# Two gated networks: 12 of 22 gate/up units as seven block products, the gate-up product kept in float32

## The reference, cut to what matters

```
def swiglu(x, wg, wu, wd):
    return (jax.nn.silu(x @ wg) * (x @ wu)) @ wd

h = h + 0.5 * swiglu(rmsnorm(h, ffn1_norm), ffn1_wg, ffn1_wu, ffn1_wd)
...                                             # mixer: attention
h = h + 0.5 * swiglu(rmsnorm(h, ffn2_norm), ffn2_wg, ffn2_wu, ffn2_wd)
gate = jax.nn.sigmoid(rmsnorm(h, ple_gate_norm) @ ple_w_gate)
e = rmsnorm(p @ ple_w_proj, ple_norm)
h = h + gate * e
```

## Time and profile before

| | us |
|---|---|
| three runs, median (lowest to highest) | 2103.69 (2100.93 to 2104.84) |
| profiled execution, span from first to last instruction | 2100.9 |
| PE busy | 2065.8 (98%) |
| weight loads busy (beside PE) | 1788.4 (85%) |
| POOL busy | 907.5 (43%) |
| VectorE busy | 854.1 (41%) |
| ScalarE busy | 717.4 (34%) |
| mean granted TensorE clock, of full speed | 0.996 |

### The profile page before, as it was taken

How to read it: one execution, slowest core, us unless ns; L and a number is a source line. 1 busy time by engine, 2 the same in 40 slices (tenths; PEclk the granted TensorE clock), 3 DMA queues, 4 the chain that set the end, 5 groups by cost and what they waited for, 6 DMA issues and landing times.

```text
span 2100.9 us, 37982 instructions
## 1 busy us (share of the span) xinstructions
PE 2065.8 (98%) x15692; PEld 1788.4 (85%) x15692; DVE 854.1 (41%) x1254; ACT 717.4 (34%) x1085; POOL 907.5 (43%) x690
## 2 busy tenths in 40 slices
PE   8999999999999999999999999999999999999998
PEld 7888888877887888887888999999999898998887
DVE  4222300577686522223008527833221546555202
ACT  5222221445687422224215432331222432222213
POOL 4444444435321444344444534435443154445542
PEclk9999999999999999999999999999999999999999
DMA  5323222431100223322322232122322123232221
GB/s 183 98 81 100 100 89 91 139 115 61 42 4 3 91 80 100 100 87 93 100 100 80 81 100 63 62 81 80 100 84 83 35 81 97 83 100 89 91 100 60
DMA packets 152360, 179.03 MB, mean 85 GB/s; under 512 B 7109, under 2 KB 142766, under 8 KB 152254
## 3 DMA queue, kind: packets, MB, share of 16 engines
q1 hardware_dynamic: 152091, 177.43, 26.0%
q10 hardware_dynamic: 163, 0.04, 0.0%
HBM read 175.37 MB, written 2.10 MB: 84 GB/s over the span
## 4 chain that ended last, share of the span: by engine, by line
PE 72%; issue 13%; POOL 8%; DVE 5%; ACT 2%; DMA 1%; SPq 0%; POOLq 0%; DVEq 0%; ACTq 0%
PE ps L2061 47%; PE ps L2202 11%; POOL wlo L734 8%; PE ps L2709 2%; PE ps L2472 1%; PE ps L2503 1%; PE ps L2483 1%; PE ps L2303 1%; DVE tmp L1396 1%; DMA raw<-in_ffn_wu 1%; DVE Q L1880 0%; DVE K L1883 0%; PE ps L2510 0%; PE ps L2610 0%; PE ps L2560 0%
## 5 line engine op out<-in xcount | busy, mean ns | idle before, releaser
L734 POOL TENSOR_TENSOR wlo<-raw,whi 128x512 fp32r<-128x512 f32 x630 | 841.8, 1368 | 1068.0 <-ACT whi L830 1067.9
L2061 PE MATMUL ps<-xh,whi 128*128 128x258 f32 (+2 forms) x2400 | 687.3, 333 | 1.0 <-POOL wlo L734 0.7
L2061 PE MATMUL ps<-xh,wlo 128*128 128x258 f32 (+2 forms) x2400 | 682.0, 331 | 0.0
L2061 PE MATMUL ps<-xl,whi 128*128 128x258 f32 (+2 forms) x2400 | 680.3, 330 | 1.4 <-issue 1.4
L830 ACT ACTIVATE whi<-raw 128x2048 fp32r<-128x2048 f32 (+1 forms) x158 | 301.3, 1907 | 770.0 <-PE ps L2061 479.3
L2061 PEld LDWEIGHTS ps<-xh,whi 128*128 128x128 f32 x2400 | 406.7, 189 | 52.5 <-issue 3.1
L2061 PEld LDWEIGHTS ps<-xh,wlo 128*128 128x128 f32 x2400 | 405.6, 188 | 45.3 <-issue 1.9
L2061 PEld LDWEIGHTS ps<-xl,whi 128*128 128x128 f32 x2400 | 405.4, 189 | 45.4 <-issue 1.6
L2202 PE MATMUL ps<-act_h,wlo 128*128 (+1 forms) x528 | 208.6, 395 | 0.0
L2202 PE MATMUL ps<-act_l,whi 128*128 (+1 forms) x528 | 208.6, 395 | 0.0
L2202 PE MATMUL ps<-act_h,whi 128*128 (+1 forms) x528 | 208.6, 395 | 0.0
(11 more groups left out here) (358 smaller groups left out, 2324.9 us busy)
## 6 DMA issues: line engine op xcount, KB each, us to landing
raw<-in_w_in SPq DMA_DIRECT2D x47, 1024.0 KB, 5.0
raw<-in_ffn_wu SPq DMA_DIRECT2D x22, 1024.0 KB, 5.3
raw<-in_ffn_wd SPq DMA_DIRECT2D x22, 1024.0 KB, 4.9
raw<-in_w_up SPq DMA_DIRECT2D x22, 1024.0 KB, 5.1
raw<-in_ffn_wg SPq DMA_DIRECT2D x21, 1024.0 KB, 5.3
raw<-in_w_down SPq DMA_DIRECT2D x11, 1024.0 KB, 4.9
raw<-in_w_out SPq DMA_DIRECT2D x8, 1024.0 KB, 5.0
raw<-in_ple_w_gate SPq DMA_DIRECT2D x4, 1024.0 KB, 4.9
```

What stands on the lines that cost most here:

```text
L734: last = nc.gpsimd.tensor_tensor(wlo[:, slot, d], raw[:, slot, d], whi[:, slot, d].bitcast(F32), ALU.subtract)
L2061: last = mm(ps[:, j * banks + b, 0:n], w[:, k, e * P:(e + 1) * P], x[:, k, c0:c0 + n], start=(k == 0 and q == 0), stop=(k == KD - 1 and q ...
```

## The change

Twelve of the 22 up-stage units of each of the first two networks are computed as a 2 x 2 block product with seven block products instead of eight. The blocks are the upper and lower half of the 1024 features, the two column groups of 128 of the unit, and the two halves of the 512 tokens. A block product is 4 row tiles x 3 products of 256 columns, so a unit is 84 matmuls of 256 columns. Four sums of weight blocks are formed per unit by VectorE (in float32, in `wlo`'s place), four sums of activation blocks once per network, from float32 copies `xf` of the scaled activations; all are then split into rounded part and remainder. The order of units is two opening units, two direct ones, then six times two of seven and one direct.

`whi` and `wlo` become a ring of eight pieces of 512 columns, handed on piece by piece; a direct unit has four pieces, one of seven has seven. In a unit of seven, VectorE forms six of the seven remainders and POOL one. The gate-up product stays in float32 (`act_f`), two tiles in one instruction, and is split in the down stage into a ring of four places (`acth2`, `actl2`). All loops of these stages are written out. The embedding's transposes move into the tenth up unit. Some semaphores are merged and buffers moved.

```diff
+HI_ORDER = (0, 3, 1, 2, 4, 5, 6)
+LO_ORDER = (6,)
+PATTERN = "DD" + "SSD" * 6
 # SP: load(u) still waits lo_ready >= u - 1; one unit number is skipped behind each network
+SKIPPED = (W_IN1 - 1, W_PLG - 1)
 # POOL
+            def seven_lo(f, u):
+                for j in LO_ORDER:
+                    pool.wait_ge(*rounded_piece(f, u, j))
+                    nc.gpsimd.tensor_tensor(block_of(wlo_f, f, u, j), src, block_of(whi_f, f, u, j).bitcast(F32), ALU.subtract)
 # ScalarE
+            def sums_rounded(f):
+                act.wait_ge(sum_made, 8 * f.g + 4)
+                for i in range(4):
+                    nc.scalar.activation(sumh[:, i], sums[:, i], ACT.Copy).then_inc(xf_ready, 1)
+            def kept(f, u, what):
+                act.wait_ge(piece_done, PIECE_DONE[u, (0, 2, 4)[what]])
+                if what == 1:
+                    ins = nc.scalar.activation(sc[:, v % 2, 1:3, :], ps[:, b + 2:b + 4, 0:HS], ACT.Copy)
+                else:
+                    ins = nc.scalar.activation(sc[:, v % 2, 3 if what else 0, :], ps[:, b, 0:HS], ACT.Copy)
+            def up_period(f, i):
+                if after in ("seven", "direct"):
+                    (seven_hi if after == "seven" else direct_hi)(f, u + 1, 0)
+                if this == "seven":
+                    kept(f, u, 0)
+                    kept(f, u, 1)
+                if after == "seven":
+                    seven_hi(f, u + 1, 3)
+                elif after == "direct":
+                    direct_hi(f, u + 1, 1)
+                    direct_hi(f, u + 1, 2)
+                if i % 2:
+                    silu_pair(f, i // 2)
+                if after == "seven":
+                    seven_hi(f, u + 1, 1)
+                    seven_hi(f, u + 1, 2)
+                elif after == "direct":
+                    direct_hi(f, u + 1, 3)
+                if this == "seven":
+                    kept(f, u, 2)
+                if after == "seven":
+                    for j in (4, 5, 6):
+                        seven_hi(f, u + 1, j)
 # ScalarE, first opening
             for n in range(KD):
                 square_of(0, n, h[:, n, M:T], M)
-            hi_one(2)
+            for n in range(KD):
+                xf_of(n, "ffn1_norm")
+            sums_rounded(FFNS[0])
             ...                                  # ten DMA issues
             root(0, 1)
-            hi_one(3)
             ...                                  # copies of the turned rows
-            ffn_up(0, W_UP1, ahead=1)
+            ffn(FFNS[0])                         # begins with direct_hi(2, 0..3), silu_pair(0)
 # ScalarE, second opening
+            def pass_on_f(n):
+                pass_on(2, 2, n, xh, "ffn2_norm", M)
+                xf_of(n, "ffn2_norm")
+            square(W_OUT1, pass_on_f)            # ends with hi_one(W_UP2 + 1)
+            sums_rounded(FFNS[1])
-            hi_one(W_UP2 + 2)
             root(2, 1)
 # ScalarE, between up and down of the second network
+                acth_pair(f, 0); acth_pair(f, 1)
+                down_hi(f, f.downs[0], c)        # c = 0, 1
+                between()                        # 8 copies of e, 8 squares
+                for d in range(11):
+                    acth_pair(f, d + 2)
+                    down_hi(f, f.downs[d + 1], c)
 # VectorE
+            def x_sums(f):
+                dve.wait_ge(xf_ready, (KD + 4) * f.g + KD)
+                nc.vector.tensor_tensor(t[0], part(0, 1), part(0, 0), ALU.subtract)
+                nc.vector.tensor_tensor(t[1], part(1, 1), part(0, 1), ALU.subtract)
+                nc.vector.tensor_tensor(t[2], part(1, 1), t[0], ALU.subtract)
+                nc.vector.tensor_tensor(t[3], part(1, 0), t[2], ALU.subtract)
+            def x_rests(f):
+                for i in range(4):
+                    dve.wait_ge(xf_ready, (KD + 4) * f.g + KD + i + 1)
+                    nc.vector.tensor_tensor(suml[:, i], sums[:, i], sumh[:, i].bitcast(F32), ALU.subtract)
+            def up_period(f, i):
+                taken_of(f, i - 1)
+                if after == "seven":
+                    for j in (1, 2, 4):
+                        seven_sum(f, u + 1, j)   # each waits until its piece is free
+                if i % 2 == 0:
+                    prod_pair(f, i // 2 - 1)
+                if after == "seven":
+                    for j in (0, 3, 1, 2):
+                        seven_rest(f, u + 1, j)
+                if this == "seven":
+                    seven_begun(f, u)            # two combinations of 256 columns
+                if after == "seven":
+                    seven_sum(f, u + 1, 5)
+                    for j in (4, 5):
+                        seven_rest(f, u + 1, j)
+            # seven_taken: 512 and 256 columns out of PSUM, then 1024 columns times rbs
             for n in range(1, KD):
                 add_square(0, n, M)
+            x_sums(FFNS[0])
+            x_rests(FFNS[0])
             rsqrt(0, 1)
             keep_spread(0, True)
-            ffn_up(0, W_UP1)
+            ffn(FFNS[0])
 # PE
+            def seven(f, i):
+                banks_free(f, i)
+                for j in range(7):
+                    pe.wait_ge(*split_piece(f, u, j))
+                    if j in (4, 5):
+                        pe.wait_ge(seven_kept, 3 * v + j - 3)
+                    for c in range(4):
+                        for q, (w, x) in enumerate(((wh, xs[0]), (wl, xs[0]), (wh, xs[1]))):
+                            last = mm(out_, w[:, c, :], x[:, c, :], ...)     # 256 columns
+                    last.then_inc(piece_done, 1)                             # the seventh: tiles_done
-            ffn_up_rest(0, W_UP1)
-            ffn_down(0, W_DN1)
+            ups(FFNS[0])
+            downs(FFNS[0], last_taken(FFNS[0]))
```

More of the change, by code:

```diff
@@ new lines, with piece_counts, count @@
+FFNS = (Ffn(0, W_UP1, 0), Ffn(1, W_UP2, 1))
+def piece_counts():
+    hi, lo, rest, total, done = {}, {}, {}, {}, {}
+    def count(table, keys):
+        at_ = table["n"] = table.get("n", 0) + 1
+        for key in keys:
+            table[key] = at_
+    for f in FFNS:
+        for u in range(f.first, f.end):
+            if f.kind(u) == "seven":
+                for j in HI_ORDER[:-1]:
+                    count(hi, [(u, j)])
+                for j in LO_ORDER[:-1]:
+                    count(lo, [(u, j)])
+                for j in REST_ORDER:
+                    count(rest, [(u, j)])
+                for j in SUMS:
+                    count(total, [(u, j)])
+                for j in range(6):
+                    count(done, [(u, j)])
+            elif f.kind(u) == "direct":
+                for j in range(3):
+                    count(hi, [(u, j)])
+                    count(lo, [(u, j)])
+                    count(done, [(u, j)])
+            elif f.kind(u) == "down":
+                count(hi, [(u, 0), (u, 1)])
+                for j in range(3):
+                    count(lo, [(u, j)])
+    return hi, lo, rest, total, done
@@ L643, in up @@
                 s = first % 2
[L644 to L648 removed]
+                with sp.Fori(0, F // UC) as i:
                     load(first + 2 * i, s, KD, wa(i * UC))
@@ L658, in down, with ffn @@
                         load(first + 1 + 2 * i + e, (s + 1 + e) % 2, 2, w[:, bass.ds(2 * i + 1 + e, 1)].rearrange("p u k n -> p (u k) n"))
+            def ffn(f, wa, wb, wd, beside=None):
+                gate, up_ = col_unit(wa), col_unit(wb)
+                rows = a[wd][0].rearrange("(u k p) n -> p u k n", p=P, k=2)
+                for u in range(f.first, f.end):
+                    if f.kind(u) in ("open", "direct", "seven"):
+                        if u >= 2:
+                            load(u, u % 2, KD, (up_ if (u - f.first) % 2 else gate)((u - f.first) // 2 * UC))
+                        if u == 2:
+                            constants_in()
+                    elif f.kind(u) == "down":
+                        load(u, u % 2, 2, rows[:, f.side(u)])
+                    else:
+                        beside(u)
             def square(first, name):
@@ new lines, in embed_lo, with ffn_lo @@
+            def embed_lo(f, u):
+                pool.wait_ge(hi_ready, u + 1)
+                for j in range(4):
+                    last = nc.gpsimd.tensor_tensor(piece(wlo_f, f, u, j), raw[:, u % 2, j * PIECE:(j + 1) * PIECE],
+                                                   piece(whi_f, f, u, j).bitcast(F32), ALU.subtract)
+                last.then_inc(lo_ready, 1)
+            def ffn_lo(f, u0, u1):
+                for u in range(u0, u1):
+                    if f.kind(u) == "seven":
+                        seven_lo(f, u)
+                    elif f.kind(u) == "direct":
+                        direct_lo(f, u)
+                    elif f.kind(u) == "down":
+                        down_lo(f, u)
+                    elif f.kind(u) == "embed":
+                        embed_lo(f, u)
+                    else:
+                        lo(u, u % 2)
@@ new lines, in up_period @@
```

(19 more changed lines are left out.)

517 lines of the change are left out of this document (389 added, 128 removed).

## The result

The changed kernel takes 2091.0 us (median of four runs, 2089.5 to 2093.9) against 2103.1 before, a ratio of 0.9944 with a 95% interval of 0.9931 to 0.9958: 12.1 us or 0.56% faster. The forecast was 2094.0. The profiled execution was measured at 2091.44 us with a span of 2089.7, so 1.7 us lie around the span. Its mean granted clock is 0.992, for 0.996 before.

A forecast was written before the change was run, and what follows sets the result against it. PE was taken as the bound. Gains and losses, 27.7 - 14.9 - 2.2 + 0.2 = 10.8 us, less 1.1 gave 9.7: span 2091.2, plus 2.8 around it, 2094.0 us; own range 2088 to 2100, 8 of 10 within 2079 to 2112.

The forecast's parts named there:

- What bounds it: Whole kernel: PE, busy 2065.8 of 2100.9 us; only fewer or shorter PE instructions help, new waits are paid in full.
- The product: Up stage: 84 matmuls at 0.1185 us, 9.95 us a unit, saving 1.16 each, 27.7 us in both networks.
- The other engines: Units of seven: VectorE, ScalarE and POOL feed PE in time, least slack 1.7 us, costing nothing.
- rival C: Pairs of sevens: VectorE becomes the bound through late remainders; 2136 us, with half of it 2115; chance 0.19.
- First opening: First network: PE waits 8.6 us at the spread, 2.7 before unit 2, plus 3.6 for the clock: 14.9 us lost.
- Second opening: Second network: sums' chain stays hidden, but PE waits for POOL's late remainder of unit 1: 2.2 us lost.
- Embedding and down stage: After the embedding POOL's first down pieces cost 0.5 us, the embedding's 0.7 us wait goes: 0.2 us gained.
- The 1.1 us for semaphore waits: Sum: 1.1 us given back for 24 x 7 semaphore waits at PE that may not all be free.
- The 2.8 us around the span: Profiled span to measured time: 2.8 us taken to lie around the span, from 2100.9 against the median 2103.7.
- A2: Openings take all: first costs 17.5 us, second 7, matmuls come at 0.1202 us; 2103 us; chance 0.14.
- B: Hardly any stall: block sums ready before the spread, all but 2 us of the gain arrives; 2078 us; chance 0.10.

The follow-up runs named there:

- e8: Changed kernel with the same twelve sevens a network in three runs of four instead of six pairs, embedding one place earlier: 2091.9 us, 0.9933 of before.
- e10: e6 with sixteen sevens a network instead of twelve, in a run of four and one of twelve: 2066.5 us, 0.9816 of before.
- e3: Changed kernel with unit 2's rounding ahead of the rounding of the activation sums in the first opening: 2091.05 us.
- e7: Changed kernel with all seven remainders of a seven-product unit on POOL instead of one: 2094.7 us, 0.9951 of before.
- e6: e4 with unit 2's rounding before the first network's root, and the second network's embedding and second-down-unit roundings earlier: 2072.7 us, 0.9843 of before.
- e4: Changed kernel with root first in both networks, activation sums, roundings and remainders after period 2, first network's scaled copies after the root: 2079.0 us, 0.9883 of before.
- e1: Changed kernel with no sevens: every gate/up unit direct, no activation block sums, roundings or remainders: 2110.1 us, 1.0028 of before.
- e2: Changed kernel with four sevens a network instead of twelve, openings untouched: 2115.2 us, 1.0052 of before.

## Why the prediction was right, step by step

**What bounds it.** Right. PE is 98% busy before and after, every wait that went or came moved the end of the network it stood in, and 312 us more of work on VectorE and ScalarE moved nothing outside the two openings, the embedding and the second down unit.

**The product.** Right in kind, too small in size. I took 0.1185 us a matmul from a stream of another stage; the sevens run at 0.1172 (why the two streams differ is not shown), 9.80 us a unit for my 9.95. Saved are 1.31 us a unit for 1.16, 31.4 us in all for 27.7. That term is the largest single error of the sum, 3.7 us.

**The other engines.** Right, almost to the instruction. The heaviest case, a seven with the 1024-column product and another seven behind it, is the unit from 76.55 to 86.34. VectorE's timeline:

```profile
84.10 1.29 DVE L1781 TENSOR_TENSOR wlo<-raw,whi 128x512 fp32r<-128x512 f32 x2
...
87.77 1.48 DVE L1781 TENSOR_TENSOR wlo<-wsum,whi 128x512 fp32r<-128x512 f32 x2
```

The first piece is done at 84.79, 1.55 us before PE enters the next seven at 86.34; I had 8.3 for 9.95, 1.7 us of slack. The last remainder ends at 89.25, 12.7 us after the unit's start where I had 13.1, and PE needs it at 93.33. In the list of PE's waits the sevens have no line. The chance of 0.19 for rival C was too high: e8 and e10 show room for sixteen.

**First opening.** Four of its sizes can be read off. The spread: forecast 41.4, measured 42.00, with the chain in the order given, instruction by instruction, and 0.6 us later because the scaled copies began 0.6 later (26.31 for 25.71, by the late start of the opening). Wait at the spread 8.06 for 8.6. Second wait 2.70 for 2.7. Clock 4.8 us lost for 3.6: 2.3 behind the first wait (1.73 us from the spread to the next matmul, 0.81 of it usual, and 4.28 us from there to the turned rows, 2.86 before) and 2.5 behind the second, to which I had given half a chance. Together 15.6 for 14.9, and network 1 ends 0.7 us later than before for my 1.

**Second opening.** Wait 1.55 for 2.2. POOL ran from 736.98 to 744.46 where I had 736.6 to 744.1, because the two engines took turns as I worked out; timeline of POOL, then VectorE's:

```profile
736.98 7.48 POOL L879 TENSOR_TENSOR wlo<-raw,whi 128x512 fp32r<-128x512 f32 x4 [8.28 <-ACT whi L1019]
```

```profile
735.26 1.22 DVE L1789 TENSOR_TENSOR sums<-xf 128x1024 f32<-128x1024 f32 x1
736.39 1.22 DVE L1790 TENSOR_TENSOR sums<-xf 128x1024 f32<-128x1024 f32 x1
737.53 2.33 DVE L1792 TENSOR_TENSOR sums<-xf,sums 128x1024 f32<-128x1024 f32 x1
739.89 2.20 DVE L1794 TENSOR_TENSOR sums<-xf,sums 128x1024 f32<-128x1024 f32 x1
```

The two sums that meet POOL from their start take 2.33 and 2.20 us for 1.22, and POOL 7.48 for 5.04. The sum of 736.39 came first: POOL begins at 736.98 beside it, and it takes its 1.22 us all the same. So the later one waits; two engines at half speed would have slowed that sum too. PE's row behind the wait:

```profile
744.51 0.50 PE L2508 MATMUL ps<-xh,whi 128*128 128x512 f32 x1 [1.55 <-POOL wlo L879]
```

What I missed is that PE would come late: it needs POOL's pieces at 742.96 where I had 741.5. Of these 1.4 us 0.7 are there when the first network's down stage ends (383.8 for 383.0), and 0.7 come in the attention part between. POOL is 0.4 later, and 2.6 less 1.1 is the 1.5 measured. The Trainium skill ("SBUF — State Buffer", "Who interferes with whom") calls this an exclusive lock between a VectorE instruction with two SBUF inputs and a GpSimd instruction that reads SBUF. These rows, e3 and e7 agree, down to the passes over `ps` that are spared. That its rule speaks against moving remainders to VectorE was no objection: that move takes them off POOL, and e7 shows the lock at its worst where they are put back.

**Embedding and down stage.** Wrong in sign, small. I had the two cancel with 0.2 us gained; they are 1.44 and 0.72 us against 0.67 before, 1.5 us lost. The failed step is "the split is made many units earlier": the activation's is, but the weights' rounding still stood last in ScalarE's queue, behind the closing work of the unit, and e6 removed both by moving it.

**The 1.1 us for semaphore waits** were unneeded: no wait of PE shows inside the sevens. The 2.8 us around the span were 1.1 too many, for 1.7 us lie there. The sum's errors stand so, to my 9.7 us: +3.7 (pitch), -0.7 (first opening), +0.65 (second), -1.7 (embedding), +1.1: 12.75, with 11.2 measured. Of the 1.5 us between, 0.9 are the late start before the spread and 0.7 come in the attention part between the networks, neither of which I had. So the mechanism is right in its large terms, and that the total comes within 1.5 us of the span is in part luck: errors of 5.4 us one way and 4.0 the other.

**The rivals.** A2 was out by its first condition, the sums of opening 2 stayed hidden. B's time, 2078, was right for a kernel that was not this one: e4, the same products with the sums out of the root's way, takes 2079.0.

## What to carry to other kernels

When a product gets cheaper by preparing its operands, look first at the place where the preparation enters an in-order queue: here 15.6 of 31.4 us saved went to two stalls and the half clock behind them, and moving the same instructions behind the one that PE was waiting for gave 12.0 us back (some 2.4 of them, by the profiled execution, because the clock stayed up behind a wait), three more moves another 6.3. A preparation whose first use is many microseconds away goes behind everything with a nearer due time, and a rounding that another engine's work depends on goes ahead of a unit's closing work. Before limiting an optimisation for fear of a second engine, read its busy time, and PE's waits, in a stretch that has nothing else: sixteen units fitted where twelve were used.

## What the runs showed of the hardware that I had not expected

- The same 2.70 us wait at the same place of PE's stream brought the clock down in the changed kernel, e1 and e8 (the next twelve matmuls take 5.26 us for 2.9), in e2 for a part (3.99), and not in e4 and e7. Such a stall may or may not cost 2.4 us more; behind the long one at the spread (7.7 to 11.1 us) the clock was at 0.50 each time, in the changed kernel, e2, e3, e7 and e8.
- In e7 VectorE and POOL were busy 25.5 and 29.45 us of 31, 55 us together, and PE did not wait. Where both have operands in the on-chip memory, an instruction's row grows by its wait for the other (689 to 1278 ns), and that counts as busy: a busy share near 1 on such a pair is no proof that it is the bound.
- Edits in the first two networks moved the stages behind them by 2 to 6 us: in waits of PE that the profile leaves unnamed (e2, e10) and in further stretches at the lower clock (e3, e10). What a stage's edit is worth is better read at the end of that stage, and two profiled executions are better compared with their granted clocks beside them.
